# A decoder step on one Trainium2 core: gate inputs and sample states in column groups, key and query norms as scalars per token, last inverse level on its corner

## What is computed

```
h = rmsnorm(x);  u, qkv, z, b, a = split(h @ w_in)
pool: causal means of u over windows 2, 4, 8, 16, minus u, times a matrix per group
q, k, v = silu(causal depthwise conv of width 4 over qkv)
q = q * rsqrt(sum(q*q) + eps) * 128**-0.5;  k = k * rsqrt(sum(k*k) + eps)     (per token and head)
beta = sigmoid(b);  g = -exp(a_log) * softplus(a + dt_bias)
delta rule in chunks:  A = I + strict(beta k k^T * decay);  [w, u] = A^-1 [beta k exp(g_cum), beta v]
    v_new = u - w S;  o = (q exp(g_cum)) S + (q k^T * decay) v_new;  S = S exp(g_last) + k_dec^T v_new
o = o * rsqrt(mean(o*o) + eps) * dn_norm * silu(z);  x += [pool, o] @ w_out
x += top-4-of-32 mixture of experts (three 1024x1024 matrices each);  x += (p @ w_ple) * sigmoid(rmsnorm(x) @ w_ple_gate)
y = rmsnorm(x);  returned too: the new pool, conv and delta-rule states
```

## Time and profile before

| | |
|---|---|
| runs (3) | 1289.27 to 1290.70 us, median 1290.07 |
| profiled execution | 1288.88 us, span 1287.2 us |
| PE busy | 1216.1 us (94%) |
| weight loads of the PE | 537.1 us (42%) |
| VectorE busy | 403.2 us (31%) |
| ScalarE busy | 207.1 us (16%) |
| GpSimd busy | 33.5 us (3%) |
| HBM traffic | 429.54 MB read, 4.11 MB written |

### The profile page before, as it was taken

How to read it: one execution, slowest core, us unless ns; L and a number is a source line. 1 busy time by engine, 2 the same in 40 slices (tenths; PEclk the granted TensorE clock), 3 DMA queues, 4 the chain that set the end, 5 groups by cost and what they waited for, 6 DMA issues and landing times.

```text
span 1287.2 us, 14674 instructions
## 1 busy us (share of the span) xinstructions
PE 1216.1 (94%) x5617; PEld 537.1 (42%) x5633; DVE 403.2 (31%) x734; ACT 207.1 (16%) x353; POOL 33.5 (3%) x106
## 2 busy tenths in 40 slices
PE   6998899999999999999999989999999999999996
PEld 5665887463333333333333323333333333332342
DVE  3656556457231303122121303031221303030333
ACT  3344241222011001010110000010100100000134
POOL 4001200000000000000000000000000000000000
PEclk8998899979999999999999989999999999999998
DMA  9931201458999999999999999999999999999801
GB/s 293 333 126 66 80 1 35 140 201 332 390 429 427 429 428 429 429 428 429 428 429 429 428 427 428 427 427 429 428 428 429 428 429 428 428 428 426 338 1 41
DMA packets 47828, 434.71 MB, mean 338 GB/s; under 512 B 6360, under 2 KB 13413, under 8 KB 23201
## 3 DMA queue, kind: packets, MB, share of 16 engines
q1 hardware_dynamic: 41641, 430.75, 80.4%
q10 hardware_dynamic: 6144, 3.39, 1.0%
HBM read 429.54 MB, written 4.11 MB: 337 GB/s over the span
## 4 chain that ended last, share of the span: by engine, by line
PE 71%; DMA 18%; DVE 5%; issue 2%; ACT 2%; POOL 1%; SPq 0%; DVEq 0%; ACTq 0%; PEldq 0%; POOLq 0%
PE ps L1365 36%; DMA ring<-in_w_up 18%; PE ps L1394 7%; PE ps L1282 5%; PE ps L975 4%; PE ps L1028 4%; PE ps L1093 4%; PE ps L1192 2%; PE ps L1176 2%; DVE x_resid L1610 1%; PE ps L1354 1%; PE ps L1183 1%; PE ps L1108 1%; PE ps L1306 1%; PE ps L1506 1%
## 5 line engine op out<-in xcount | busy, mean ns | idle before, releaser
L1365 PE MATMUL ps<-ring,ht_region 128*64 128x512 f32 (+1 forms) x2176 | 456.4, 602 | 16.6 <-DMA ring<-in_w_up 16.6
L1365 PEld LDWEIGHTS ps<-ring,ht_region 128*64 128x64 f32 (+1 forms) x2176 | 149.2, 135 | 310.1 <-issue 310.1
L1365 PE MATMUL ps<-ring,q_region 128*64 128x512 f32 (+1 forms) x1088 | 223.2, 594 | 0.0
L1961 DVE TENSOR_SCALAR q_region<-ps 128x1024 f32<-128x1024 f32 x16 | 19.6, 1225 | 369.3 <-PE ps L1365 369.1
L1365 PEld LDWEIGHTS ps<-ring,q_region 128*64 128x64 f32 (+1 forms) x1088 | 71.7, 134 | 144.2 <-issue 144.2
L1394 PE MATMUL ps<-u_region,h_region 128*128 128x512 f32 (+1 forms) x192 | 93.6, 621 | 0.0
L1028 PE MATMUL ps<-ht_region,ring 128*128 128x320 f32 x320 | 93.3, 451 | 0.3 <-PE ps L1028 0.3
L1968 DVE TENSOR_SCALAR q_region<-ps 128x1024 f32<-128x1024 f32 x16 | 19.6, 1225 | 211.8 <-PE ps L1365 211.8
L1949 DVE TENSOR_TENSOR x_resid<-ps,x_resid 128x512 f32<-128x512 f32 (+1 forms) x96 | 66.1, 689 | 40.1 <-PE ps L1394 38.3
L1028 PEld LDWEIGHTS ps<-ht_region,ring 128*128 128x128 f32 x320 | 63.5, 199 | 27.9 <-issue 4.7
L881 ACT ACTIVATE ht_region<-ps 128x512 f32<-128x512 f32 x32 | 19.2, 599 | 259.0 <-PE ps L1282 259.0
(11 more groups left out here) (368 smaller groups left out, 918.1 us busy)
## 6 DMA issues: line engine op xcount, KB each, us to landing
ring<-in_w_gate SPq DMA_DIRECT2D x64, 2048.0 KB, 26.6
ring<-in_w_up SPq DMA_DIRECT2D x64, 2048.0 KB, 18.6
ring<-in_w_down SPq DMA_DIRECT2D x64, 2048.0 KB, 22.8
ring<-in_w_in SPq DMA_DIRECT2D x5, 2048.0 KB, 19.9
ring<-in_w_out SPq DMA_DIRECT2D x2, 2048.0 KB, 11.9
ring<-in_w_ple_gate SPq DMA_DIRECT2D x1, 4096.0 KB, 24.6
x_resid<-in_x_prompt SPq DMA_DIRECT2D x4, 512.0 KB, 3.9
out<-ring ACTq DMA_DIRECT2D x1, 2048.0 KB, 9.9
```

Source lines behind the costliest of these rows:

```text
L1365: ins = mm(PS[s0_:s0_ + width, b0 + hf, :], lhs[:, k, s0_:s0_ + width], w[a_][:, kk, hf * 512:(hf + 1) * 512], start=False, stop=(k == KT ...
```

## The change

It does four things. Gate inputs: `w_in`'s last columns become the weights, padded with zeros to 32 columns; k-tiles go to four column groups of the PE array (`tile_position`), all 320 tokens moving, and three small matmuls with a selecting matrix (`sel8`) add the groups and turn them to tokens. Norms: k and q are no longer normed; the eight sums of squares go to one bank in column groups, are turned to one scalar per token and head, and enter into beta (`bet2`), into the evacuation of v (`rinv`) and into the output norm (`qeps`). Sample states: packed keys and queries are the weights, the states move in four column groups, and 16 small DMAs on ScalarE's queue bring the rows to their tokens in place of the PE's turning. The last level of the inverse works on its 64x64 corner alone. Pool products 0 to 2 are put ahead of the turned conv states.

```diff
-            for t, (t0, n) in enumerate(TILES):
-                for k in range(KT):
-                    last = mm(ps[0:n, t * 8:(t + 1) * 8], hT[:, k, t0:t0 + n], wtail[:, k, :],
-                              start=(k == 0), stop=(k == KT - 1))
+            mm(ps[:, 0:T], zerob[:, 0:P], zerob[:, 0:T], start=True, stop=False, skip_group_check=True)
+            for k in range(KT):
+                c0 = 32 * (k % 4)
+                last = mm(ps[c0:c0 + 32, 0:T], wtail[:, k, :], hT[:, k, :], start=False, stop=(k >= 4),
+                          tile_position=(0, c0), skip_group_check=True)
+            def token_scalars(name, src, pick):
+                ps = fill(name)
+                for t, (t0, n) in enumerate(TILES):
+                    last = mm(ps[0:n, t * 8:(t + 1) * 8], src[:, t0:t0 + n], pick, start=True, stop=True)
+            def sums(ps, half):
+                for h in range(HEADS):
+                    last = mm(ps[32 * h:32 * h + 32, 0:T], onesab[:, half, :], sqb[h], start=False, stop=(half == 1),
+                              tile_position=(0, 32 * h), skip_group_check=True)
...
-            for b in IN_ORDER[:2]:
-                for c in range(4):
-                    project(4 * b + c)
+            project(8)
+            pe.wait_ge(v_mark, VM["bat"])
+            token_scalars("bar", bat, sel8[:, :])
+            for c in (9, 10, 11, 4, 5, 6, 7):
+                project(c)
             for i in range(8):
                 project(VU[i])
-                ps = fill(f"ss{i}")
-                pe.wait_ge(sq_ready, i + 1)
-                mm(ps[:, 0:T], ones[:, :], sqb[i % 2], start=True, stop=True).then_inc(fsem(f"ss{i}"), 1)
+                if i == 0:
+                    nps = fill("nkq")
+                    mm(nps[:, 0:T], zerob[:, 0:P], zerob[:, 0:T], start=True, stop=False, skip_group_check=True)
+                    pe.wait_ge(sq_ready, 4)
+                    sums(nps, 0).then_inc(sq_used, 1)
+                if i == 2:
+                    pe.wait_ge(sq_ready, 8)
+                    sums(nps, 1).then_inc(fsem("nkq"), 1)
+                if i == 4:
+                    pe.wait_ge(v_mark, VM["nkq"])
+                    token_scalars("tok", nkq, ident[:, 0:P:16])
...
-            for h in range(HEADS):
-                for b in range(DB):
-                    last = mm(ps[:, h, :, b * DS:(b + 1) * DS], s0[:, b, h, :], ct[:, h:h + 5:4, c:c + DS],
-                              start=True, stop=True)
+            for r in range(2):
+                ps = fill(f"kqs{r}")
+                for h in range(HEADS):
+                    for j in range(4):
+                        last = mm(ps[32 * j:32 * j + 32, h * P:(h + 1) * P], kqc[:, h, (4 * r + j) // 2],
+                                  s0[:, 4 * r + j, h, :], start=True, stop=True, tile_position=(0, 32 * j))
...
+                    if s == LEVELS - 1:
+                            last = mm(ps[64:P, h * P:h * P + 64], sc[2][0:64, h, 64:P], sc[4][0:64, h, 0:64],
+                                      start=True, stop=True)
...
-                if s == 2:
-                    for nm, q in (("R2k", 1), ("R2q", 0)):
-                            last = tr(ps[0:NSAMP, h * P:(h + 1) * P], kqS[:, h, q * NSAMP:(q + 1) * NSAMP])
```

ScalarE:

```diff
-                if i:
-                    norm_root(i - 1)
-                if i + 2 < 8:
-                    square(i + 2)
-            norm_root(7)
+                if i in (1, 2):
+                    square(2 * i + 2)
+                    square(2 * i + 3)
+            act.wait_ge(v_mark, VM["tok"])
+            step(a.activation(rinv, norms[:, :, 0::2], ACT.Sqrt), a_mark, AM["rinv"])
...
+            for r in range(2):
+                copy(kqS[:, r], bank(f"kqs{r}"), f"kqs{r}")
+            for r in range(2):
+                for j in range(4):
+                    for q in range(2):
+                        p0 = 32 * j + 16 * q + 8 * (j % 2)
+                        b = 4 * r + j
+                        act.dma_start(kqrow[b * DS:(b + 1) * DS, q], kqS[p0:p0 + DS, r]).then_inc(kq_rows, 16)
```

VectorE:

```diff
+            is_filled(dve, "ba")
+            drain(v.tensor_copy(bat, bank("ba")[:, 0:T]), "ba")
+            mark(v.memset(oss[:, 0:1], 0.0), "bat")
             dve.wait_ge(bias_in, 16 * 3)
...
-            for i in range(8):
-                if i < 4:
-                    conv(8 + i)
-                c = NORMED[i]
-                is_drained(dve, f"ss{i}")
-                step(v.reciprocal(rnb[i % 3], rnb[i % 3]))
-                step(v.tensor_tensor(ct[:, c, :], ct[:, c, :], rnb[i % 3], ALU.mult), norm_ready)
+            conv(8)
+            conv(9)
+            is_filled(dve, "nkq")
+            drain(v.tensor_copy(nkq, bank("nkq")[:, 0:T]), "nkq")
...
+            conv(10)
...
+            conv(11)
...
-                    is_filled(dve, "R2k")
-                    step(v.tensor_tensor(oN[2], ps4("R2k", NSAMP, P), over(egc[0:NSAMP, 2, :], HEADS, P), ALU.mult))
+                    dve.wait_ge(kq_rows, 16 * 16)
+                    step(v.tensor_tensor(oN[2], rows[1], over(egc[0:NSAMP, 2, :], HEADS, P), ALU.mult))
```

More of the change, by code:

```diff
@@ L375, in trunk_kernel @@
                 nxt(f"pr{4 * b + c}")
+                if 4 * b + c == 8:
+                    nxt("bar")
         nxt("gcs")
@@ L379, in trunk_kernel @@
             nxt(f"pr{VU[i]}")
-            nxt(f"ss{i}")
-        for n in ["pr16", "npp", "nps", "pr17", "pr18", "pr19", "cnp0", "cnp1", "cnp2", "cns0", "cns1", "cns2"]:
+            if i in (0, 4):
+                nxt(("nkq", "", "", "", "tok")[i])
+        for n in ["pr16", "npp", "nps", "pr17", "pr18", "pr19", "cnp0", "cnp1", "cnp2", "pm0", "pm1", "pm2",
+                  "cns0", "cns1", "cns2", "pm3"]:
             nxt(n)
-        for g in range(PG):
-            nxt(f"pm{g}")
         for t in range(NT):
@@ L388, in trunk_kernel @@
             nxt(f"qk{t}")
-        for n in ["kqs", "T0", "kN0", "kN1", "kN2", "T1", "vN0", "vN1", "vN2", "T2"]:
+        for n in ["kqs0", "kqs1", "T0", "kN0", "kN1", "kN2", "T1", "vN0", "vN1", "vN2", "T2"]:
             nxt(n)
@@ L762, in _ @@
                     prev.append(c - 4)
-            square(0)
-            square(1)
+            for i in range(4):
+                square(i)
             silu_conv(prev.pop(0))
@@ L804, in _ @@
             for t, (t0, n) in enumerate(TILES):
-                copy(vN[0:n, t], bank(f"vN{t}")[0:n, :].rearrange("p (h d) -> p h d", h=HEADS), f"vN{t}")
-            is_filled(act, "kqs")
+                nm = f"vN{t}"
+                is_filled(act, nm)
+                for h in range(HEADS):
+                    last = h == HEADS - 1
+                    step(a.activation(vN[0:n, t, h], bank(nm)[0:n, h * P:(h + 1) * P], ACT.Copy, scale=rinv[0:n, t, h:h + 1]),
+                         dsem(nm) if last else None, uses[nm][1] + 1 if last else None)
             for h in range(HEADS):
@@ L1075, in _, with pool_product @@
                 last.then_inc(fsem(f"cnp{i}"), 1)
+            def pool_product(g):
+                pe.wait_ge(d_ready, g + 1)
+                ps = fill(f"pm{g}")
+                mm(ps[:, 0:SEQ], poolw[:, g, :], prompt_cols(ue, g, PH), start=True, stop=True)
+                mm(ps[:, SEQ:T], poolw[:, g, :], sample_cols(ue, g, PH), start=True, stop=True
+                   ).then_inc(fsem(f"pm{g}"), 1)
+            pe.wait_ge(poolw_in, 16)
+            for g in range(PG - 1):
+                pool_product(g)
             for i in range(3):
@@ L1133, in _ @@
                         is_drained(pe, f"QT{s - 1}{t}")
+                    if s == LEVELS - 1:
+                        ps = fill(f"P{s}{t}")
+                        for h in range(HEADS):
+                            last = mm(ps[64:P, h * P:h * P + 64], sc[2][0:64, h, 64:P], sc[4][0:64, h, 0:64],
+                                      start=True, stop=True)
+                        last.then_inc(fsem(f"P{s}{t}"), 1)
+                        continue
                     per_head(f"P{s}{t}", n, n, lambda h: sc[2][:, h, :], lambda h: sc[4][:, h, :])
@@ L1603, in _ @@
             mark(v.tensor_tensor(kdec[:, :, :], egl[:, :, :], gc[:, :, :], ALU.subtract), "gcs")
-            for i in range(8):
-                if i < 4:
-                    conv(8 + i)
-                c = NORMED[i]
-                is_drained(dve, f"ss{i}")
-                step(v.reciprocal(rnb[i % 3], rnb[i % 3]))
-                step(v.tensor_tensor(ct[:, c, :], ct[:, c, :], rnb[i % 3], ALU.mult), norm_ready)
+            conv(8)
+            conv(9)
+            is_filled(dve, "nkq")
+            drain(v.tensor_copy(nkq, bank("nkq")[:, 0:T]), "nkq")
+            mark(v.memset(oss[:, 0:1], 0.0), "nkq")
+            conv(10)
+            is_filled(dve, "tok")
+            for t, (t0, n) in enumerate(TILES):
+                ins = v.tensor_scalar(norms[0:n, t], bank("tok")[0:n, t * 8:(t + 1) * 8], EPS, None, ALU.add)
+                drain(ins, "tok") if t == NT - 1 else step(ins)
```

(6 more changed lines are left out.)

129 lines of the change are left out of this document (71 added, 58 removed).

## The result

| | before | after | difference |
|---|---|---|---|
| time, median of the runs measured side by side (4 each) | 1289.67 us | 1268.05 us | ratio 0.984, 95% interval 0.9824 to 0.9856 |
| the profiled execution: its time | 1288.88 us | 1267.36 us | -21.5 |
| its span | 1287.2 us | 1265.6 us | -21.6 |
| mean granted TensorE clock | 0.972 | 0.981 | |

The forecast was 1265, with a range of 1258 to 1273. The time lies in the range, 3 us above the forecast. Four points of the profiled executions say where the 21.6 us come from: the start of the gate sums ("gcs", the small matmuls behind the first eight projections), of the decay matmuls (G), of the first inverse product (P10) and of the first value product (v0).

A forecast was written before the change was run, and what follows sets the result against it. The expert loop was bound by its weight stream, which starts only after a front of PE, VectorE and ScalarE work. -16.3 - 7.7 + 1.5 - 2.7 + 0.2 = -25.0 from 1288.88 gives 1263.9, forecast as 1265, range 1258 to 1273.

The forecast's parts named there:

- What bounds the kernel: Expert loop runs at its weight stream's pace; ahead of it DMA idles, so time saved in front moves the end equally.
- Rival D: Whole kernel: no effect on the end, the weight stream being the true bound and startable no earlier; 1290 us, chance 0.02.
- Gate inputs, -4.7: Start of the front: column-grouped matmuls replace 24 small ones, -5.4 us, the new "bar" adds 0.7; half clock left as is.
- rival C: First projections and before P10: half-clock stretches fall away with denser work; 1261 us, chance 0.12.
- Squares and norms, -9.6: First such projection to end of the ninth: 53.7 us becomes 44.0, including a 2.2 us PE wait for squares.
- pooling, -2.0: Pooling before G: VectorE, free of reciprocals, starts earlier, so the PE bounds; 2.0 us saved.
- Sample states, -7.7 up to P10: G to P10: grouped products at 84 ns a record take 5.4 us, VectorE then bounds; ScalarE's issues, 5.6 us, just fit.
- rival B: Gate inputs, square sums and sample-state products: column groups don't overlap; about 1277 us, chance 0.05.
- rival A: ScalarE's queue before P10: issues cost 0.72 us, P10 waits, 6.5 us come back; 1271.5 us, chance 0.12.
- The clock of the inverse, +1.5: Inverse's first level: PE gaps ahead of P10 may leave it at 1.2 GHz; 1.5 us charged, bounds 0 and 4.
- Rival E: Inverse: the PE never gets back to 2.4 GHz, +34 us on -25; about 1299 us, chance 0.03.
- Inverse, -2.7: P10 to first value product: R2 transposes go -0.9, VectorE's wait goes -0.7, last level on the corner -1.1 us.

The follow-up runs named there:

- run 7: Changed kernel with the gate inputs as before (24 matmuls over 8 columns, no column groups): 1273.25 us.
- run 1: Changed kernel with the 16 sample-row transfers issued on SyncE's queue instead of ScalarE's: 1265.34 us.
- run 3: Changed kernel with the four squares of the queries computed together, ahead of the silu that waits for VectorE: 1267.77 us.
- run 5: The changed kernel measured again, without an edit: 1270.18 us.
- run 10: Changed kernel with squares early, the 16 transfers on ScalarE behind the vN copies, and the three operations on the sample rows moved from VectorE to GpSimd: 1257.49 us.
- run 8: Changed kernel with the norms of keys and queries as before (ones product, root, 320-column reciprocal, product per head): 1279.11 us.
- run 4: Changed kernel with the squares of the queries early and the 16 transfers on SyncE's queue: 1260.94 us.
- run 6: Changed kernel with the squares of the queries early and the 16 transfers on ScalarE behind the vN copies: 1260.14 us.
- run 2: Changed kernel with the 16 transfers still on ScalarE, but moved behind its 12 vN copies: 1262.72 us.
- run 12: Changed kernel with the inverse's last level at its full 128 columns as before: 1267.91 us.

## Why the prediction was right, and where it was off

- **What bounds the kernel.** Right. v0 to the end is 1077.3 us after and 1077.5 before. Rival D is out.
- **Gate inputs, -4.7.** Right in the work (1.28 and 0.29 us for "ba", 0.72 for "bar"), too small in the effect: gcs came 7.5 us earlier in the profiled execution. The step that failed is "I leave that as it is", of the half clock in the first projections, some 2.4 us. It came back with the 24 small products (run 7) and was gone, or shorter, without them; this much of rival C came true. In runs 1, 3, 5 and 10 gcs came 1.9 to 3.4 us later than in the first profile, so -7.5 is its best value.
- **Squares and norms, -9.6, and pooling, -2.0.** Right in kind and nearly in size: 9.8 against 11.6 in the profiled pair, 8.9 for the norms alone in run 8. The term that was mis-sized is the wait for the squares of the queries, 3.45 us for 2.2. In seven other profiles with the squares in that place it was 3.15, 3.26 and five times 2.30, so 2.2 is near its lower end; what moves it was not taken apart. It is ScalarE's order of work and no price of the hardware, as runs 4 and 6 show, where gcs to G is 64.19.
- **Sample states, -7.7 up to P10.** The rule that set it was right: without ScalarE in the way VectorE's masks bound P10, and G to P10 is 19.61, for 20.1 by the forecast. The new product was taken too dear, 84 ns a record; it took 57 ns in the profiled execution and 30 in run 5 (1.95 us for 64), but it lies beside VectorE's work. So rival B is out: the column groups overlap. What failed is **"I take 0.35, since 8 plain rows are nearest to the former: 5.6 us, kN0 free at about 160, just in time"**. An issue took 0.66 us and all 10.63. This is the mechanism of rival A, whose sign in the list of what would be wrong ("a ScalarE issue stretch over 8 us with P10 idle behind it") stands in the profile. It cost 4.8 us in front of P10 (24.40 to 19.61; 3.1 in runs 7 and 12, where the products and transposes ahead ran at full clock) and 2.2 behind it. The reading under the 0.35 was wrong already in the trace of the kernel before. The 0.31 of the earlier trace rows is the cheapest of five single transfers that stand next to each other on that queue:

```profile
137.98 0.58 ACTq L794 DMA_DIRECT2D out<-ring  x1
138.61 0.31 ACTq L795 DMA_DIRECT2D out<-ring  x1
138.95 0.38 ACTq L796 DMA_DIRECT2D out<-ring  x1
139.37 0.73 ACTq L797 DMA_DIRECT2D out<-ring  x1
140.13 0.75 ACTq L798 DMA_DIRECT2D out<-in_state_pool  x1
```

Their mean is 0.55 us, and with the bias pieces at 0.72 the rows spoke for 9 to 12 us of issue, so rival A deserved more than 0.12. What makes one transfer dearer to issue than another was not taken apart; it is not the target alone, since the transfers at 0.31 and 0.73 are both stores to the kernel's outputs.

- **The clock of the inverse, +1.5.** Right in kind: P10's first 4.9 us ran at 0.52, 2.15 us over run 2, where P10 waits for nothing and has 1.00 throughout. It was put down to the gaps of the new products; run 2 has these gaps too and keeps 1.00, so the wait for ScalarE is what brings it. Rival E did not occur; after 4.9 us the clock was back, though run 5 has further half-clock stretches in the levels.
- **Inverse, -2.7.** Right: 38.10 against 40.86 at full clock, 2.76. Of it the corner is 1.2 (run 12) for 1.1.
- **Landing, issuing, switching.** The landing was covered, as taken: in run 10 the last rows lay ready 1.5 us behind the last issue, and no landing was part of the path. The Trainium skill (DMA: Bandwidth & Descriptors, Anatomy of one DMA) gives a transfer a fixed cost of 2 us, fitted for transfers that GpSimd issues; these lay ready a little sooner. The Trainium skill (DMA: Bandwidth & Descriptors, Issuing engines are not separate DMA queues) says that issuing on several engines only saves the time to initiate a DMA, "which is usually small relative to the DMA itself". The first half agrees with run 1. The second does not hold for transfers of this size: that time was 0.66 us times 16 on the engine for which P10 waited, against 1.5 us from the last issue to the rows' being ready. The price of a switch was read too dear, since a record's length holds more than its work (a single ones-matmul is 0.70 us long and costs 0.54). From start to start, four sums in column groups took 0.68 us (62.94 to 63.62), 0.13 over their 0.55, so two switches cost at most that. The Trainium skill (TensorEngine Tiling, Key Properties) states a drain at each; the trace shows no more of it than this.

Together: -25.0 was forecast, -21.6 measured. At the gate inputs 2.8 us more came than forecast, most of it the clock of the first projections; the issues (some 5 us with their half clock, beyond the 1.5 charged) and the longer wait for the squares took it back and more. So the number is better than the mechanism: what happened is rival A's mechanism with a part of rival C's gain, each given 0.12. That the two misses lie on opposite sides is luck.

## What to carry to other kernels

Count a DMA's issue as an instruction of the engine that issues it, at the price of the row in the trace that is most like it, and ask what stands behind it in that queue: 16 small transfers were free as data and cost 7 us as issues, and moving six lines of code down gave these back. When the gap before P10 went, the slow clock behind it went too (runs 1, 2, 4, 6 and 10), so a wait is worth more than its length (4.8 us and 2.2 behind it here). When rows of one kind cost 0.31 to 0.75 us, take their spread and not the cheapest. And when single executions differ by 6 us, cut each trace at the same four or five points, and compare only the stretch that the edit touches; a difference in a stretch that no edit touches says how far the others can be believed.

## What the hardware showed that was not expected

- A transfer of 8 rows of 2 KB from SBUF to SBUF took 0.66 us to issue on ScalarE and 0.68 on SyncE; with 4 rows 0.62. Half the bytes saved next to nothing. Five single transfers of other shapes on ScalarE's queue took 0.31 to 0.75.
- 64 matmul records of 32 columns over 128, in four column groups, took 1.95 us at full clock (30 ns each) and 3.5 to 3.6 at a granted clock of about 0.53 in other executions of the same code. By the rate of the projections (0.545 us for 320 columns) 32 such products one after the other would take 7.0 us, a quarter of it 1.74, so the column groups overlapped fully with f32 operands.
- The place of the half-clock stretches is not a property of the program. In code that no edit touched, the projection behind the gate sums took 4.57 us in some executions and up to 7.6 in others. In three (runs 1, 3 and 5), the products of "ba", at 18.9 us, took nearly twice their usual time (2.36 for 1.28) while the granted clock in that stretch reads 1.00. Why is open.
